# Making the gate-times-gelu products of a group of experts behind the dot products of the next group

## The reference

```python
gate = jax.nn.softmax(top_s, axis=-1)
act = jax.nn.gelu(jnp.einsum('thed,td->the', U[idx], xt).astype(jnp.float32), approximate=False)
return jnp.einsum('the,thed->td', (gate * act).astype(V.dtype), V[idx])
```

## Time and profile before

| | |
|---|---|
| runs of before | 2206.45 and 2202.4 us, median 2204.43 us |
| the profiled execution | 2211.82 us, of it 2210.0 us span |
| busy share of the span | TensorE 84%, VectorE 65%, GpSimd 60%, ScalarE 21% |
| first and last U gather of a tile's group | issued at 794.0 and 2161.5 us |
| last layer norm done | about 2208 us |

### The profile page before, as it was taken

How to read it: one execution, slowest core, us unless ns; L and a number is a source line. 1 busy time by engine, 2 the same in 40 slices (tenths; PEclk the granted TensorE clock), 3 DMA queues, 4 the chain that set the end, 5 groups by cost and what they waited for, 6 DMA issues and landing times.

```text
span 2210.0 us, 20632 instructions
## 1 busy us (share of the span) xinstructions
PE 1853.2 (84%) x6794; PEld 993.2 (45%) x6794; DVE 1434.1 (65%) x3330; ACT 463.6 (21%) x1122; POOL 1331.9 (60%) x1280
## 2 busy tenths in 40 slices
PE   8999787787758848899978889978999987899886
PEld 7844476686522423344533333523444543335332
DVE  1256456656651267788578787587787677787665
ACT  1132200000000012332223332223233222122220
POOL 0012355545337047777777777777777777777774
PEclk9999787687669879999988999998999998999888
DMA  5120222122039159999999999999999999999997
GB/s 196 58 81 16 79 63 60 50 63 62 20 117 361 32 214 399 409 409 387 379 383 409 402 405 382 386 376 394 407 379 402 364 388 397 409 406 381 409 382 283
DMA packets 177642, 618.85 MB, mean 280 GB/s; under 512 B 20372, under 2 KB 23828, under 8 KB 177152
## 3 DMA queue, kind: packets, MB, share of 16 engines
q0 software_dynamic: 160000, 578.89, 68.2%
q1 hardware_dynamic: 17536, 38.64, 4.8%
HBM read 611.79 MB, written 5.59 MB: 279 GB/s over the span
## 4 chain that ended last, share of the span: by engine, by line
PE 22%; POOL 18%; DMA 12%; DVE 8%; issue 6%; ACT 1%; SPq 0%; DVEq 0%; POOLq 0%
PE ps L1564 16%; DMA p_Ur<-in_peer_u_dram,p_idx 11%; POOL p_Ur L1398 9%; POOL p_Vr L1398 8%; DVE p_Ur L1777 4%; PE ps L1518 2%; PE ps L1492 1%; ACT p_dg L1668 1%; PE ps L1462 1%; ACT p_gel L1662 0%; PE ps L1579 0%; PE ps L1464 0%; DVE p_wgt L1786 0%; DVE p_x L1703 0%; DVE p_x L1707 0%
## 5 line engine op out<-in xcount | busy, mean ns | idle before, releaser
L1564 PE MATMUL ps<-p_Vr,p_dg 128*128 128x512 f32 x2048 | 996.9, 644 | 198.8 <-ACT p_dg L1668 198.6
L1777 DVE CUSTOM_DVE_ANT_0 p_Ur<-p_Ur,p_x 128x1024 f32<-128x1024 f32 x512 | 616.8, 1225 | 252.5 <-DMA p_Ur<-in_peer_u_dram,p_idx 242.7
L1564 PEld LDWEIGHTS ps<-p_Vr,p_dg 128*128 128x128 f32 x2048 | 411.0, 206 | 748.8 <-issue 495.3
L1398 POOL DMA_INDIRECT p_Ur<-in_peer_u_dram,p_idx x512 | 517.5, 1011 | 233.1 <-issue 155.7
L1398 POOL DMA_INDIRECT p_Vr<-in_peer_v_dram,p_idx x512 | 539.8, 1054 | 161.3 <-issue 122.7
L1662 ACT ACTIVATE p_gel<-p_dot 128x4 f32<-128x4 f32 x128 | 26.3, 205 | 935.4 <-DVE p_dot L1777 935.4
L1668 ACT ACTIVATE p_dg<-table_long,p_wgt 128x128 f32<-128x128 f32 x512 | 163.6, 390 | 29.3 <-DVE p_wgt L1786 29.1
L379 POOL TENSOR_TENSOR am<-kk,am 128x536 f32<-128x536 f32 x4 | 7.4, 1850 | 213.4 <-DVE wq L443 213.4
L760 POOL DMA_INDIRECT kr<-in_cache_k_dram,idx x64 | 62.5, 977 | 89.3 <-DVE sc L807 73.9
L254 PE MATMUL ps<-xT,w_ring 128*128 128x268 f32 x448 | 103.9, 396 | 6.7 <-DMA xT<-in_xT_dram 6.7
L767 POOL TENSOR_TENSOR kr<-kr,w_out 128x512 f32<-128x512 f32 x64 | 81.9, 1311 | 44.0 <-DMA kr<-in_cache_k_dram,idx 44.0
(11 more groups left out here) (345 smaller groups left out, 2074.1 us busy)
## 6 DMA issues: line engine op xcount, KB each, us to landing
w_ring<-in_w_in_dram SPq DMA_DIRECT2D x5, 2048.0 KB, 8.2
p_Ur<-in_peer_u_dram,p_idx POOLq DMA_INDIRECT x512, 6.6
p_Vr<-in_peer_v_dram,p_idx POOLq DMA_INDIRECT x512, 6.7
w_out<-in_w_out_dram SPq DMA_DIRECT2D x1, 4096.0 KB, 20.2
wq<-in_pk_wq_dram SPq DMA_DIRECT2D x1, 4096.0 KB, 39.7
xT<-in_xT_dram SPq DMA_DIRECT2D x4, 536.0 KB, 6.5
w_out<-q_rows SPq DMA_DIRECT2D x8, 256.0 KB, 3.6
p_x<-in_x_tok_dram SPq DMA_DIRECT2D x4, 512.0 KB
```

What stands on the lines that cost most here:

```text
L1398: pool.indirect_dma_start(out=dst, out_offset=None, in_=io[table], in_offset=bass.IndirectOffsetOnAxis(ap=at, axis=0)).then_inc(s_to, 16)
L1564: mm = pe.matmul(acc[:, a, :], dg[:, j % DG, :], Vr[:, j % RV, a * 512:(a + 1) * 512], start=(at == 0), stop=(at == SLOTS - 1), skip_group ...
L1777: ins = dve.tensor_tensor_reduce(Ur[:, r, :], Ur[:, r, :], x, 1.0, 0.0, ALU.mult, ALU.add, dot[:, r:r + 1])
```

## The change

Four things change. VectorE's product of gate and gelu for group g-1 (a new function `weights`) is issued after the four dot products of group g, where it was issued for group g after those of group g and a wait for its gelu. The products of the very last group (127) are made after the whole schedule. The wait for the gelu stands with the product (in the rest of 8 tokens it is written out there, so nothing changes in it). In `schedule`, `eng_head(NT, 1, 0)` stands behind the gather of g = 28 of the last tile and not ahead of it. ScalarE, TensorE and GpSimd run the code they ran before, the size of every ring is as before, and no data or arithmetic is different.

```diff
             for t in range(NT):
                 for g in range(GR):
+                    eng_gather(t, g // GPP, g % GPP)
                     if t == NT - 1 and g == 28:
                         eng_head(NT, 1, 0)
-                    eng_gather(t, g // GPP, g % GPP)
                     if t and g < 3:
...
                 ins.then_inc(s_dot, 1)
+
+            def weights(g):
+                t, at = divmod(G * g, SLOTS)
+                hs = slice(G * g % R, G * g % R + G)
                 dve.wait_ge(s_gel, g + 1)
+                dve.tensor_tensor(wgt[:, hs], gel[:, hs], gate[:, t % 2, at:at + G], ALU.mult).then_inc(s_w, 1)
 
             def gather(t, part, grp):
                 g = (PARTS * t + part) * GPP + grp
-                hs = slice(G * g % R, G * g % R + G)
-                at = TOPK * part + G * grp
                 dots(g, x1[:, t % 2, :])
-                dve.tensor_tensor(wgt[:, hs], gel[:, hs], gate[:, t % 2, at:at + G], ALU.mult).then_inc(s_w, 1)
+                if g:
+                    weights(g - 1)
...
             schedule(gather, finish, attend, head, prep)
 
+            weights(PARTS * NT * GPP - 1)
             dve.wait_ge(s_repc, 1)
             for half in range(2):
                 g = PARTS * NT * GPP + half
                 hs = slice(G * g % R, G * g % R + G)
                 dots(g, junk[:, :])
+                dve.wait_ge(s_gel, g + 1)
                 if half == 0:
                     dve.wait_ge(s_rs, 32)
```

## The result

The changed kernel takes 3143.48 us (3142.29 and 3144.67), against 2204.43 before: 1.423 times as long, 95% interval 1.418 to 1.428. It lies inside the stated range, 78 us above the forecast of 3065. The profiled execution has a span of 3140.5 us.

The account below looks back on a forecast made before the run. GpSimd's gather issue was taken as the bound, with the DMA engines full beside it. 2210 + 749 (longer loop) + 113 (side work over edges) = 3072 us of span, 3065 us expected; range 2860 to 3260.

Parts of the forecast that it names:

- The bound of before and its slack: GpSimd issues gathers without pause, 10.7 us per group; the V ring loop takes 16.6 of 21.4 us over two groups.
- The first term: V ring loop of 16.6 us goes round once per group against 10.7 us of GpSimd issue, 127 times: 749 us.
- last dot product to TensorE's start: From the start of VectorE's last dot product through product and `dg` to TensorE, gelu already there: 1.93 us.
- first slot and hand-over: TensorE's first four matmul records of a group with the hand-over to the V gather: 3.6 us, bounds 1.9 and 3.9.
- V gather and three U gathers: GpSimd's issue of four gathers until the fourth U gather starts: 5.0 us, or 5.3 by the mean times.
- fourth U gather to its dot product: From issue to landing, fifth gather in a burst, dot product starting at once: 6.1 us, bounds 5.9 and 8.1.
- The second term: VectorE meets TensorE's late side work over a group's edge, ahead of its next dots: 113 us, bounds 40 and 200.
- the maxima: VectorE's side work on TensorE's scores, 4 per tile in three tiles, 4.6 us too late each: 55 us.
- The gain that was not there: VectorE's 37.1 us wait for the gelu goes but passes to the next U row, gaining nothing.
- Idle time of GpSimd put down to TensorE: Profile sign: GpSimd's idle time before V gathers (line 1564) rises from 37 to some 600 to 800 us.
- the short loop: Rival: TensorE stays at 2.4 GHz and U rows land sooner, period 14.7 to 15.2 us, about 2860 us; chance 0.17.
- The long one: Rival: landing 8.1 us or TensorE low for whole groups, period 18 us or more, about 3290 us; chance 0.14.

Follow-up runs that it names:

- The dose: V ring of 6 rows instead of 7 (`RV = 6`), in both kernels: the changed kernel 3378.03 us, the kernel before 2225.36 us.
- the queue's order: Changed kernel with GpSimd's four U gathers of group g+1 issued ahead of the four V gathers of group g: 2439.85 us, ratio 1.103.
- the pair of runs with 23 late groups: Kernel before, product late in 23 of 128 groups only: where TensorE's side work feeds VectorE's in the next group, 2453.98 us; elsewhere, 2385.37 us.

## Why the prediction was right

**The bound of before and its slack.** The circle through the V ring had slack because it turned once in two groups. The dose shows it: one row less costs some 15 us there and 235 in the changed kernel. That GpSimd's issue was the bound is less sure than I wrote. A gather behind a gather takes 1.24 us in the burst below, eight 9.9, and the period was 10.65 with the DMA engines full (1.01). No run tells the two apart; the forecast needs only the period.

**The first term, 749 us forecast.** The mechanism is shown by two independent cuts, the queue's order (704 us back) and the ring's size (235 us more for one row). The period was 17.06 us on average, not 16.6. Step by step, over the 96 plain periods:

| step | forecast | measured (mean) |
|---|---|---|
| last dot product to TensorE's start | 1.93 | 1.34 to the `dg`, 0.46 more: 1.80 |
| first slot and hand-over | 3.6 | 3.95, mostly 4.04 |
| V gather and three U gathers | 5.0 | 4.99 |
| fourth U gather to its dot product | 6.1 | 6.32 |
| sum | 16.6 | 17.06 |

The step that was mis-sized is TensorE's first slot. I took 3.6 us with its hand-over, though the chain of before gave 3.79 and 0.13; I had averaged it down towards four matmuls at half rate. It is 3.79 and about 0.26. With the landing, which took 0.2 us longer than the forecast, and less the 0.13 us that the first step was shorter, that makes 0.46 us in a period and about 58 us in 127. The landing had the right source: the first gathers into an empty queue, not the stream's median. In the changed kernel the five gathers of one burst, from 2014.9 us on, landed after 4.2, 5.1, 5.5, 6.2 and 6.3 us. The rule of the Trainium skill (DMA: Bandwidth & Descriptors, "Anatomy of one DMA — SWDGE (gpsimd) path") is stated for one DMA; taken for each gather by itself it would give the fifth the time of the first. The rows decide against that here, it holds for the first alone.

**The second term, 113 us forecast.** The profile has 112 us in the 23 periods that were named, 4.9 each. By kind the sums are near too: the maxima 58 us (55 forecast), the attention's copy 8 (11), the projection 27 (31), the scale behind it 19 (16). Single ones are less so: the maxima take 19.0 to 24.7 us where 21.2 was forecast for all, so part of the agreement is that of an average. VectorE's waits for TensorE's scores, projection and norm are the 144.6, 52.1 and 46.1 us above. I called it a sum of its own, and the pair of runs with 23 late groups bears that out: there too a period at an edge is 5.0 us longer than one elsewhere, though the time differs by only 3.0 us for each. The 12 us in the five other long periods were not in the forecast. With the 58 us they make up what the span of 3140.5 us lies above the 3072 forecast (68.5), to within 2 us.

**The gain that was not there.** The 37.1 us of waiting for the gelu did go, and the time went to the wait for U rows, as argued. The run with the products ahead of the dots hides the gelu as well and is 130 us slower than before.

**What I said the profile would show.** Idle time of GpSimd put down to TensorE 600 to 800 us: it was 982.8. My figure held only the first term, and the edges and the longer loop stand in the same place. DMA share 0.65 and 255 GB/s: 0.66 and 234. Starts 16.6 us apart: 17.1. The rivals: the short loop would have needed the fast first slot, which came in one of the 96 plain periods (15.3 us long). The long one needed a landing near 8 us, and the fourth U gather's was 6.32.

## What to carry to other kernels

Before an operation is put off by one step of a pipeline, follow what it releases until you come back to where you began, in-order queues included, and count how many periods one turn of that circle may take. If putting it off turns two periods for a turn into one, the whole length of the circle becomes the period, whatever the busy shares say. Look in particular for a queue in which the next step's loads stand behind a wait for an old buffer.

## What the runs showed of the hardware that I had not expected

With seven matmuls of no use put ahead of most groups, TensorE's first slot still was slow (1.2 GHz) in 35 of 96 plain periods, 27 of them with such matmuls ahead. The idle time right before a group does not tell which. Behind 2.23 us it was slow (8.83 us for the group), behind 1.75 us fast (7.13), but also behind 3.23 us (the same kernel's timeline):

```profile
2100.18 7.13 PE L1570 MATMUL ps<-p_Vr,p_dg 128*128 128x512 f32 x16 [3.23 <-ACT p_dg L1674]
```

In 20 more periods the clock was kept up, but the matmuls ended too late and gave most of the gain away. Work put in to keep the clock up did so only in part.

Behind a pause, the time of an indirect gather of 512 KB to its landing climbs from 4.2 to 6.3 us within five gathers and stays there (6.2 to 6.4 for the next three), while they are issued 1.24 us apart or more. The DMA engines, busy 0.66 of the time on average, are close to full within such a burst (busy time by stretch, the columns as above, the burst begins at 2014.86):

```profile
2014.86:2017.50 2.64, 2.64 (x8) 1.21 (x7) 0.00 (x0) 0.00 (x0) 2.03 (x3) 1.00 0.36 70
2017.50:2020.00 2.50, 2.23 (x6) 0.69 (x4) 0.00 (x0) 0.00 (x0) 1.89 (x3) 1.00 0.88 320
2020.00:2022.00 2.00, 0.00 (x0) 0.00 (x0) 0.69 (x1) 0.00 (x0) 1.70 (x2) 1.00 0.97 326
```

So the mean share of a stretch hides that the later gathers of a burst meet busy engines. That this is why they land later is likely and not shown.
